# A three-mixer block on one core: the q, k projection with its two token parts side by side, and VectorE gating retention's outputs

## The chip, the cores and the metric

The kernel runs on one core of one Trainium2 chip. The time is device microseconds (us) of that core for one execution. The engines are TensorE (PE, with PEld for its weight loads), VectorE (DVE), ScalarE (ACT), GpSimd (POOL) and SyncE (SP), which here only issues DMAs.

## What is computed

256 tokens of width 1024 pass through a gated delta-net layer, a short-convolution layer, and then the second block, in which the change lies. Cut to what matters:

```python
proj = h @ w_in[l]                       # h: 256 x 1024
q, k, v, z_ret, u_val, u_gate, z_conv, g_a, g_b = jnp.split(proj, split_at, axis=-1)
qh = rotary(q.reshape(B, S, RET_HEADS, RET_HEAD_QK).astype(jnp.float32), positions)
kh = rotary(k.reshape(B, S, RET_HEADS, RET_HEAD_QK).astype(jnp.float32), positions) * RET_HEAD_QK ** -0.5
vh = v.reshape(B, S, RET_HEADS, RET_HEAD_V).astype(jnp.float32)
ret = head_groupnorm(retention_chunkwise(qh, kh, vh)).reshape(B, S, RET_V_DIM).astype(x.dtype)
y_a = (ret * jax.nn.silu(z_ret)) @ w_ret_out[l]
a = u_val * jax.nn.sigmoid(u_gate)
a = causal_depthwise_conv_2(a, conv_w[l], conv_b[l])     # 31 taps, 1024 channels
a = jax.nn.silu(layernorm(a, conv_ln_g[l], conv_ln_b[l]))
y_b = (a * jax.nn.silu(z_conv)) @ w_conv_out[l]
merged = jax.nn.sigmoid(g_a) * y_a + jax.nn.sigmoid(g_b) * y_b
```

## The kernel before

The weights stream in as chunks of 1 MB (`w_raw`), and every projection is a phase of such chunks, in the order of `PHASES`: ..., glu (8 chunks), qk (8), v (8), zret (8), zconv (4), gates (8), ret_out (8), conv_out (4), w_out (4). Products are made in float32 accuracy from three passes of float32r: each weight w and each activation h is kept as a high part and the rest (`w_hi`, `w_lo`, `hT_hi`, `hT_lo`), and PE adds w_hi·h_hi + w_hi·h_lo + w_lo·h_hi.

For each chunk, in two halves, ACT copies `w_raw` into `w_hi` (`split_hi`, line 1220), DVE subtracts to get `w_lo` (`split_lo`, line 1786), and PE multiplies. There are four half slots of each, so ACT's split of a half waits until PE is done with the same half two chunks earlier (`half_done`); DVE's split waits for ACT's (`hi_ready`), and PE's pass with `w_lo` waits for DVE's (`lo_ready`). In its program, each engine's step for chunk c first splits the second half of chunk c+1 and the first half of chunk c+2, and then does what the phase wants of chunk c (`each`).

PE has three ways to do a chunk. `chunk` (lines 677, 678, 686; phases qkv, qk, zconv) gives 16 + 16 + 16 matmuls of 256 columns, all into one PSUM bank `bank(j)`. `chunk_apart` (lines 695, 704; sc_in, glu) lets one matmul of 512 columns take `hT` high and low side by side, so that the halves land apart in two banks: 16 matmuls of 512 and 16 of 256; ACT then copies the low half out (`glu_part`) and DVE adds it. `wide_phase` and `wide_deep` (lines 727, 728, 734; v, zret, gates, ret_out ...) stream 512 weight columns, 24 matmuls of 512 for a chunk.

Between its splits DVE also does the 31-tap convolution, which is cut into 248 single operations (`conv_op`: lines 2396 and 2399, output `cv`, 128x256 each) and handed out by `conv_share(n)`: n of them in a step, until none is left. The shares by phase are written by hand: glu 22 in all, qk 3 a chunk, v 9 or 8, zret 7, zconv 8 and 5, gates 4 and then 10. After the last one DVE adds the channels up (`pair_sum`, `halves_sum`, output `ln_sum`, in the last step of gates), and PE takes the mean over them with a matmul (`layer_norm(0)`, line 1169) right behind the first chunk of ret_out; in PE's queue everything later stands behind it. POOL adds the first three channel pairs into `ln_sum` as they become ready (lines 1777, 1780).

In qk, DVE turns each chunk by the rotary angles straight out of PSUM (`rotate`: two multiplications into `rp`, one subtraction, one addition into `qkT`). PE's first matmuls on `qkT` (`scores`, line 1134) come behind the first chunk of v and wait for all eight. In zret, PE makes each head's retention outputs, DVE and ACT normalize them into `og`, and POOL multiplies `og` with the gates `zr` into `vt` (line 1773, two of 128x512 a head); in zconv PE transposes `vt` for ret_out.

Of the kernel before, what the change touches and what calls it, by code (L numbers as in the profile page):

```python
# [98 lines left out]
def build(nc, x_in, pre_norm_w, post_norm_w, gdn_w_in, gdn_conv_w, gdn_A_log, gdn_dt_bias, gdn_norm_w, gdn_w_out,  # L99
# [3 lines left out]
    with ctx:  # L103
# [146 lines left out]
        def bank(b, inner=SEQ):  # L250
            return psum[:, b, :].rearrange("p (a n) -> p a n", n=inner)
# [327 lines left out]
        def _(pe):  # L579
# [255 lines left out]
            def phase(name, a_hi, a_lo, beside=None, first=None, midway=None):  # L835

                g0 = FIRST[name]
                if name in ("sc_in", "glu"):
                    pe.wait_ge(bank_free, 4 + g0)

                def step(i):
                    for j in range(4):
                        ahead = isinstance(i, int) and i == 0
                        if ahead and j == 0 and first is not None:
                            first_chunk(g0, first)
                        elif ahead and j < 2 and midway is not None:
                            continue
                        elif name in ("sc_in", "glu"):
                            chunk_apart(i, g0, j, midway if ahead and j == 2 else None)
                        else:  # L850
                            chunk(i, g0, j, a_hi, a_lo, midway if ahead and j == 2 else None)
                        if beside is not None:
                            beside(4 * i + j)
                if beside is not None:
                    for i in range(COUNT[name] // 4):
                        step(i)
                elif midway is not None:
                    step(0)
                    with pe.Fori(1, COUNT[name] // 4) as i:
                        step(i)  # L860
                else:
                    loop(pe, COUNT[name] // 4, step)
# [263 lines left out]
            def scores(c):  # L1126

                if c == 0:
                    pe.wait_ge(rp_step, 2 * RH)
                if c < RH:  # L1130
                    b = psum[:, 4 + c, :]
                    for o, keys, queries in ((b[:, 0:SEQ], slice(0, P), slice(0, SEQ)), (b[:, SEQ:SEQ + P], slice(P, SEQ), slice(P, SEQ))):
                        for d in range(2):
                            mm = pe.matmul(o, qkT[:, KT + 2 * c + d, keys], qkT[:, 2 * c + d, queries], start=(d == 0), stop=(d == 1))  # L1134
                    mm.then_inc(sco_done, 1)
# [73 lines left out]
        def _(act):  # L1209
# [422 lines left out]
                act.wait_ge(bank_free, i * 4 + (4 + g + j - 1))  # L1632
                act.activation(glu_part[j % 2][:, :, :], psum[:, 2 * j:2 * j + 2, SEQ:2 * SEQ], ACT.Copy).then_inc(sc_act, 1)
            chunks("glu", glu_each, apart=True)
            chunks("qk")

            def tokens_out(dst, func):
                def each(i, j, done):
# [90 lines left out]
        def _(pool):  # L1729
# [36 lines left out]
            pool.wait_ge(yT_turned, KT)  # L1766
            pool.memset(ada_sum[:, :, :], 0.0).then_inc(ada_used, ADA)

            for n in range(NT * RH):
                h, t = n // NT, n % NT  # L1770
                pool.wait_ge(gn_ready, n + 1)
                vh = slice(h * RDV, (h + 1) * RDV)
                pool.tensor_tensor(vt[:, t, vh], og[t][:, :], zr[:, t, vh], ALU.mult).then_inc(rg_ready, 1)

            pool.wait_ge(rg_ready, NT * RH)
            pool.wait_ge(cv_step, CW * 4)
# [7 lines left out]
        def _(dve):  # L1784
# [655 lines left out]

            def rotate(i, j, done):
                c = 4 * i + j
                conv_share(3)
                dve.wait_ge(half_done, done)
                dve.tensor_tensor(rp1[:, :, :], bank(j), cos2, ALU.mult)
                dve.tensor_tensor(rp2[:, :, :], bank(j), sin2, ALU.mult).then_inc(bank_free, 1)
                dve.wait_ge(bank_free, 4 + FIRST["qk"] + c + 1)
                dve.tensor_tensor(qkT[:, 2 * c:2 * c + 1, :], rp1[:, 0:1, :], rp2[:, 1:2, :], ALU.subtract)
                dve.tensor_tensor(qkT[:, 2 * c + 1:2 * c + 2, :], rp2[:, 0:1, :], rp1[:, 1:2, :], ALU.add).then_inc(rp_step, 1)
                dve.wait_ge(rp_step, c + 1)  # L2450
            dve.wait_ge(bank_free, 4 + FIRST["qk"])
            chunks("qk", rotate, unroll=True)

            def decayed(i, j, done):
                c = 4 * i + j
                conv_share(9 if c < RH else 8)
                if c < RH:
                    dve.wait_ge(sco_done, c + 1)
                    dve.tensor_tensor(st[:, c, :], psum[:, 4 + c, 0:3 * P], decay[:, c, :], ALU.mult).then_inc(st_ready, 1)
# [4 lines left out]
            def group_scale(h):  # L2464
# [2 lines left out]
                dve.wait_ge(gn_rec, 2 * h + 1)  # L2467
                dve.scalar_tensor_tensor(out=gnm[:, :], in0=gmv[:, :, 0], scalar=-1.0, in1=grs[:, :], op0=ALU.mult, op1=ALU.mult).then_inc(gn_rec, 1)

            def group_norm(i, j, done):  # L2470
                n = 4 * i + j
                h, t = n // NT, n % NT
# [6 lines left out]
                if h:  # L2479
                    dve.wait_ge(gn_rec, 2 * h)  # L2480
                dve.bn_aggr(gmv[:, t, :], gst[:, t, :]).then_inc(gn_step, 1)
            chunks("zret", group_norm, unroll=True)

            def turned_pairs(i, j, done):
                if j == 0:
                    group_scale(RH - 1)
                conv_share(5 if j else 8)
                split_two(j)

            def split_two(q):  # L2490
# [16 lines left out]

            def last_pairs(i, j, done):
                c = 4 * i + j
                conv_share(10 if c else 4)  # L2510
                if c == COUNT["gates"] - 1:
                    dve.wait_ge(cv_step, CW * KT)
                    pair_sum(0, cv[:, KT - 2:KT, :], 2)
# [123 lines left out]
```

## Time and profile before

| | before |
|---|---|
| time, median of 3 runs (lowest to highest) | 838.21 us (837.5 to 838.33) |
| the profiled execution: its time / its span | 837.87 us / 836.1 us |
| PE busy | 827.8 us (99%) |
| DVE busy | 731.1 us (87%) |
| ACT busy | 500.2 us (60%) |
| POOL busy | 45.4 us (5%) |

The span runs from the first to the last instruction; 1.77 us of the execution's time lie around it. Busy time is the union of an engine's instructions. A matmul's duration contains its drain, so neighbours overlap: what a row of matmuls costs is read from the start of the first to the start of what follows. The same holds for DVE, by less than 0.1 us.

### The profile page before, as it was taken

What the parts mean: (1) busy time and instruction counts of PE and PEld (TensorE: products, weight loads), DVE (VectorE), ACT (ScalarE), POOL (GpSimd) and SP (SyncE); (2) the same over time, 40 slices, a digit from 0 to 9 for tenths busy, and PEclk for the clock granted to TensorE, in tenths of its full rate; (3) what the DMA queues carried; (4) which work ended last, traced back from release to release, by engine and by line L of the source; (5) the groups of instructions that cost most, each with busy time, mean ns of one, the idle gap of its engine ahead of it and who ended that gap; (6) DMA issues with size and microseconds to landing.
All of it is one profiled execution on the core that took longest, in us unless ns stands there. A gap on an engine that the chain in (4) does not pass through costs nothing.

```text
span 836.1 us, 13942 instructions
## 1 busy us (share of the span) xinstructions
PE 827.8 (99%) x5146; PEld 725.1 (87%) x5146; DVE 731.1 (87%) x1179; ACT 500.2 (60%) x804; POOL 45.4 (5%) x46
## 2 busy tenths in 40 slices
PE   8999999999999999999999999999999999999997
PEld 8999998789888888888888788998887798888886
DVE  7799899868877898888989979999999999988774
ACT  6899858576566555555565775333346675546743
POOL 0001101341100000000000000000001220000000
PEclk9999999999999999999999999999999999999999
DMA  9875675511875877777776656655454435564531
GB/s 277 256 253 169 211 245 174 146 38 45 278 232 179 261 262 263 257 256 252 238 257 218 221 185 213 202 184 169 155 198 151 152 118 200 186 231 171 188 115 50
DMA packets 129882, 164.13 MB, mean 196 GB/s; under 512 B 17407, under 2 KB 92199, under 8 KB 129703
## 3 DMA queue, kind: packets, MB, share of 16 engines
q1 hardware_dynamic: 129831, 163.45, 59.9%
q8 instruction: 33, 0.54, 0.3%
q14 instruction: 18, 0.15, 0.1%
HBM read 159.20 MB, written 4.23 MB: 195 GB/s over the span
## 4 chain that ended last, share of the span: by engine, by line
PE 98%; DVE 1%; DMA 1%; issue 0%; ACT 0%; DVEq 0%; SPq 0%; ACTq 0%
PE psum L695 16%; PE psum L727 14%; PE psum L728 14%; PE psum L734 14%; PE psum L704 8%; PE psum L677 6%; PE psum L686 6%; PE psum L678 6%; PE psum L1028 2%; PE psum L631 1%; PE psum L641 1%; PE psum L635 1%; PE psum L1033 1%; PE psum L915 1%; PE psum L1146 1%; PE psum L1134 1%
## 5 line engine op out<-in xcount | busy, mean ns | idle before, releaser
L1220 ACT ACTIVATE w_hi<-w_raw 128x1024 fp32r<-128x1024 f32 x255 | 266.6, 1061 | 188.2 <-PE psum L734 87.1
L1786 DVE TENSOR_TENSOR w_lo<-w_raw,w_hi 128x1024 fp32r<-128x1024 f32 x256 | 305.2, 1221 | 44.3 <-ACT w_hi L1220 42.2
L695 PE MATMUL psum<-hT,w_hi 128*128 128x512 f32 x576 | 138.9, 391 | 0.0
L695 PEld LDWEIGHTS psum<-hT,w_hi 128*128 128x128 f32 x576 | 105.4, 188 | 20.2
L727 PE MATMUL psum<-w_hi,hT 128*128 128x512 f32 x280 | 113.3, 405 | 0.0
L728 PE MATMUL psum<-w_hi,hT 128*128 128x512 f32 x280 | 109.3, 390 | 0.0
L2399 DVE SCALAR_TENSOR_TENSOR cv<-aP,par,cv 128x256 f32<-128x256 f32 x240 | 107.9, 519 | 0.0
L677 PE MATMUL psum<-hT,w_hi 128*128 128x256 f32 x432 | 107.4, 286 | 0.0
L678 PE MATMUL psum<-hT,w_hi 128*128 128x256 f32 x432 | 105.9, 283 | 0.0
L677 PEld LDWEIGHTS psum<-hT,w_hi 128*128 128x128 f32 x432 | 82.8, 192 | 0.4 <-issue 0.2
L678 PEld LDWEIGHTS psum<-hT,w_hi 128*128 128x128 f32 x432 | 82.9, 192 | 0.3 <-issue 0.2
L704 PEld LDWEIGHTS psum<-hT,w_lo 128*128 128x128 f32 x576 | 74.8, 191 | 3.3
L704 PE MATMUL psum<-hT,w_lo 128*128 128x256 f32 x576 | 76.1, 283 | 0.0
L727 PE MATMUL psum<-w_hi,yT_hi 128*128 128x512 f32 x192 | 75.8, 395 | 0.0
L734 PE MATMUL psum<-w_lo,hT 128*128 128x512 f32 x280 | 75.6, 390 | 0.0
L728 PE MATMUL psum<-w_hi,yT_lo 128*128 128x512 f32 x192 | 74.8, 390 | 0.0
L727 PEld LDWEIGHTS psum<-w_hi,hT 128*128 128x128 f32 x280 | 52.6, 188 | 12.0 <-issue 1.7
L728 PEld LDWEIGHTS psum<-w_hi,hT 128*128 128x128 f32 x280 | 52.6, 188 | 12.0 <-issue 1.7
L734 PEld LDWEIGHTS psum<-w_lo,hT 128*128 128x128 f32 x280 | 52.6, 188 | 11.2
L686 PE MATMUL psum<-hT,w_lo 128*128 128x256 f32 x432 | 60.6, 283 | 0.0
L686 PEld LDWEIGHTS psum<-hT,w_lo 128*128 128x128 f32 x432 | 55.7, 192 | 0.0
L734 PE MATMUL psum<-w_lo,yT_hi 128*128 128x512 f32 x192 | 52.7, 389 | 0.0
(341 smaller groups left out, 1108.6 us busy)
## 6 DMA issues: line engine op xcount, KB each, us to landing
w_raw<-in_w_in_dram SPq DMA_DIRECT2D x44, 1024.0 KB, 5.1
w_raw<-in_sc_w_in_dram SPq DMA_DIRECT2D x32, 1024.0 KB, 7.9
w_raw<-in_gdn_w_in_dram SPq DMA_DIRECT2D x23, 1024.0 KB, 7.1
ada<-in_w_ada_dram SPq DMA_DIRECT2D x24, 512.0 KB, 4.8
w_raw<-in_gdn_w_out_dram SPq DMA_DIRECT2D x8, 1024.0 KB, 5.5
w_raw<-in_sc_w_out_dram SPq DMA_DIRECT2D x8, 1024.0 KB, 6.4
w_raw<-in_w_ret_out_dram SPq DMA_DIRECT2D x8, 1024.0 KB, 5.1
w_raw<-in_w_conv_out_dram SPq DMA_DIRECT2D x4, 1024.0 KB, 5.1
```

Of the source, the lines that this page charges most:

```text
L677: pe.matmul(o[:, m, :], w_hi[s][:, k, mine], a_hi[:, ka, :], start=m == 0 and ka == 0, stop=False, skip_group_check=True)
L678: pe.matmul(o[:, m, :], w_hi[s][:, k, mine], a_lo[:, ka, :], start=False, stop=False, skip_group_check=True)
L686: mm = pe.matmul(o[:, m, :], w_lo[s][:, k, mine], a_hi[:, ka, :], start=False, stop=ka == KT - 1, skip_group_check=True)
L695: pe.matmul(o, w_hi[s][:, k, mine], hT[:, h * KH2 + k, :, :], start=h == 0 and k == 0, stop=False, skip_group_check=True)
L704: mm = pe.matmul(o, w_lo[s][:, k, mine], hT_hi[:, ka, :], start=False, stop=ka == KT - 1, skip_group_check=True)
L727: pe.matmul(psum[:, b + m, :], a_hi[:, ka, mine], wide(w_hi[s])[:, e, :], start=start and h == 0 and e == 0, stop=False, skip_group_check= ...
L728: pe.matmul(psum[:, b + m, :], a_lo[:, ka, mine], wide(w_hi[s])[:, e, :], start=False, stop=False, skip_group_check=True)
L734: mm = pe.matmul(psum[:, b + m, :], a_hi[:, k + 2 * h + e, mine], wide(w_lo[s])[:, e, :], start=False, stop=stop and h == 1 and e == 1, sk ...
L1028: mm = pe.matmul(b[:, a, :], left(a), right(a), start=True, stop=True)
L1220: act.activation((w_hi[half_slot(g, h)] if home is None else third_hi[half_slot(g, home)])[:, :, :], raw[slot][:, h * KH2:(h + 1) * KH2, : ...
L1786: return dve.tensor_tensor(o, whole, hi.bitcast(F32), ALU.subtract)
L2399: dve.scalar_tensor_tensor(out=cv[:, n, :], in0=src, scalar=w, in1=cv[:, n, :], op0=ALU.mult, op1=ALU.add).then_inc(cv_step, 1)
```

## The change

The qk phase goes from `chunk` to `chunk_apart`: per chunk 16 matmuls of 512 columns and 16 of 256 in place of 48 of 256, in two banks. ACT copies the low half of each chunk into `glu_part` (8 copies of 128x512), DVE adds it to the high half into `ug_sum`, and the rotary multiplications read that. The three `conv_op`s a chunk in qk are gone; the phases v and gates take them: v 8 and then 9 in place of 9 and then 8, gates 9 and then 10 to the end. The eight multiplications of `og` with `zr` go from POOL to DVE (`gated(h)`).

```diff
-                        elif name in ("sc_in", "glu"):
+                        elif name in ("sc_in", "glu", "qk"):
                             chunk_apart(i, g0, j, midway if ahead and j == 2 else None)
...
-                    pe.wait_ge(rp_step, 2 * RH)
+                    pe.wait_ge(rp_step, 4 * RH)
...
-            chunks("qk")
+            def beside_qk_2(i, j, done):
+                c, g = 4 * i + j, FIRST["qk"]
+                act.wait_ge(half_done, done)
+                act.wait_ge(bank_free, 4 + g + c - 1)
+                act.activation(glu_part[j % 2][:, :, :], psum[:, 2 * j:2 * j + 2, SEQ:2 * SEQ], ACT.Copy).then_inc(sc_act, 1)
+            chunks("qk", beside_qk_2, unroll=True)
...
-            for n in range(NT * RH):
-                h, t = n // NT, n % NT
-                pool.wait_ge(gn_ready, n + 1)
-                vh = slice(h * RDV, (h + 1) * RDV)
-                pool.tensor_tensor(vt[:, t, vh], og[t][:, :], zr[:, t, vh], ALU.mult).then_inc(rg_ready, 1)
...
             def rotate(i, j, done):
                 c = 4 * i + j
-                conv_share(3)
                 dve.wait_ge(half_done, done)
-                dve.tensor_tensor(rp1[:, :, :], bank(j), cos2, ALU.mult)
-                dve.tensor_tensor(rp2[:, :, :], bank(j), sin2, ALU.mult).then_inc(bank_free, 1)
+                dve.wait_ge(sc_act, 6 * KT - 2 + COUNT["glu"] - 2 + c + 1)
+                dve.tensor_tensor(ug_sum[:, :, :], psum[:, 2 * j:2 * j + 2, 0:SEQ], glu_part[j % 2][:, :, :], ALU.add).then_inc(bank_free, 1)
                 dve.wait_ge(bank_free, 4 + FIRST["qk"] + c + 1)
+                dve.tensor_tensor(rp1[:, :, :], ug_sum[:, :, :], cos2, ALU.mult)
+                dve.tensor_tensor(rp2[:, :, :], ug_sum[:, :, :], sin2, ALU.mult).then_inc(rp_step, 1)
+                dve.wait_ge(rp_step, 2 * c + 1)
...
-                conv_share(9 if c < RH else 8)
+                conv_share(8 if c < RH else 9)
...
+            def gated(h):
+                vh = slice(h * RDV, (h + 1) * RDV)
+                for t in range(NT):
+                    dve.wait_ge(gn_ready, NT * h + t + 1)
+                    dve.tensor_tensor(vt[:, t, vh], og[t][:, :], zr[:, t, vh], ALU.mult).then_inc(rg_ready, 1)
...
+                if n and t == 0:
+                    gated(h - 1)
...
+                if j == 0:
+                    gated(RH - 1)
...
-                conv_share(10 if c else 4)
+                conv_share(10 if c else 9)
```

DVE in the second chunk of qk, before (`cv` is a convolution operation, `w_lo` a split, the other four the rotation):

```order
L1786 TENSOR_TENSOR w_lo_59<-w_raw_52,w_hi_55 128x1024
L2399 SCALAR_TENSOR_TENSOR cv<-aP,par,cv 128x256 x3
L2445 TENSOR_TENSOR rp_168<-psum,trig 128x512
L2446 TENSOR_TENSOR rp_169<-psum,trig 128x512
L2448 TENSOR_TENSOR qkT<-rp_168,rp_169 128x256
L2449 TENSOR_TENSOR qkT<-rp_169,rp_168 128x256
```

The same place after:

```order
L1787 TENSOR_TENSOR w_lo_59<-w_raw_52,w_hi_55 128x1024
L2446 TENSOR_TENSOR ug_sum<-psum,glu_part_186 128x512
L2448 TENSOR_TENSOR rp_168<-ug_sum,trig 128x512
L2449 TENSOR_TENSOR rp_169<-ug_sum,trig 128x512
L2451 TENSOR_TENSOR qkT<-rp_168,rp_169 128x256
L2452 TENSOR_TENSOR qkT<-rp_169,rp_168 128x256
```

The three convolution operations are gone from here, and one addition has come in front of the rotation.

DVE in the fifth step of zret, before (`gst`, `gmv` are the statistics of the group norm):

```order
L2399 SCALAR_TENSOR_TENSOR cv<-aP,par,cv 128x256 x7
L2477 BN_STATS gst<-psum 128x6
L2481 BN_AGGR gmv<-gst 128x2
L1786 TENSOR_TENSOR w_lo_58<-w_raw_51,w_hi_54 128x1024
L1786 TENSOR_TENSOR w_lo_59<-w_raw_52,w_hi_55 128x1024
```

After, with a head's two multiplications ahead of the splits:

```order
L2400 SCALAR_TENSOR_TENSOR cv<-aP,par,cv 128x256 x6
L2397 TENSOR_SCALAR cv<-aP,par 128x256
L2486 BN_STATS gst<-psum 128x6
L2490 BN_AGGR gmv<-gst 128x2
L2477 TENSOR_TENSOR vt<-og_173,zr 128x512
L2477 TENSOR_TENSOR vt<-og_174,zr 128x512
L1787 TENSOR_TENSOR w_lo_58<-w_raw_51,w_hi_54 128x1024
L1787 TENSOR_TENSOR w_lo_59<-w_raw_52,w_hi_55 128x1024
```

The pair of `vt` has come from POOL's queue, once for each of the four heads.

DVE in the last two steps of gates, before (the rows of `ln_sum` are the sums that PE's mean waits for):

```order
L1786 TENSOR_TENSOR w_lo_60<-w_raw_52,w_hi_56 128x1024
L1786 TENSOR_TENSOR w_lo_57<-w_raw_49,w_hi_53 128x1024
L2399 SCALAR_TENSOR_TENSOR cv<-aP,par,cv 128x256
L1786 TENSOR_TENSOR w_lo_58<-w_raw_49,w_hi_54 128x1024
L1786 TENSOR_TENSOR w_lo_59<-w_raw_50,w_hi_55 128x1024
L2502 TENSOR_TENSOR ln_sum_189<-ln_sum_189,cv 128x512
L2506 TENSOR_TENSOR ln_sum_189<-ln_sum_189 128x256
```

After:

```order
L1787 TENSOR_TENSOR w_lo_60<-w_raw_52,w_hi_56 128x1024
L1787 TENSOR_TENSOR w_lo_57<-w_raw_49,w_hi_53 128x1024
L2400 SCALAR_TENSOR_TENSOR cv<-aP,par,cv 128x256 x10
L1787 TENSOR_TENSOR w_lo_58<-w_raw_49,w_hi_54 128x1024
L1787 TENSOR_TENSOR w_lo_59<-w_raw_50,w_hi_55 128x1024
L2400 SCALAR_TENSOR_TENSOR cv<-aP,par,cv 128x256 x10
L2515 TENSOR_TENSOR ln_sum_189<-ln_sum_189,cv 128x512
L2519 TENSOR_TENSOR ln_sum_189<-ln_sum_189 128x256
```

Ahead of the sums there stand 20 convolution operations in these two steps where there was one; over the whole gates phase it is 79 in place of 55.

## Rows read from the trace of the kernel before

**Rows 1.** The page's chain that ended last, shares by engine.

```profile
PE 98%; DVE 1%; DMA 1%; issue 0%; ACT 0%; DVEq 0%; SPq 0%; ACTq 0%
```

**Rows 2.** All of PE's waits: us in total, times, longest.

```profile
PE psum L879 <- DVE bg L2021: 1.3, 1, 1.3
...
PE psum L631 <- DVE hT L1976: 0.3, 1, 0.3
```

**Rows 3.** Timeline of PE, sc_in and qk: start, us, instructions.

```profile
329.19 3.82 PE L695 MATMUL psum<-hT,w_hi 128*128 128x512 f32 x16
...
334.75 3.82 PE L695 MATMUL psum<-hT,w_hi 128*128 128x512 f32 x16
...
521.54 0.28 PE L677 MATMUL psum<-hT,w_hi 128*128 128x256 f32 x1
...
567.62 0.40 PE L727 MATMUL psum<-w_hi,hT 128*128 128x512 f32 x1
```

**Rows 4.** Timeline of DVE, the first chunk of qk and its last end.

```profile
525.64 2.35 DVE L1786 TENSOR_TENSOR w_lo<-w_raw,w_hi 128x1024 fp32r<-128x1024 f32 x2
527.91 1.27 DVE L2399 SCALAR_TENSOR_TENSOR cv<-aP,par,cv 128x256 f32<-128x256 f32 x3
529.10 0.68 DVE L2445 TENSOR_TENSOR rp<-psum,trig 128x512 f32<-128x512 f32 x1
...
531.21 2.36 DVE L1786 TENSOR_TENSOR w_lo<-w_raw,w_hi 128x1024 fp32r<-128x1024 f32 x2
...
570.48 2.41 DVE L1786 TENSOR_TENSOR w_lo<-w_raw,w_hi 128x1024 fp32r<-128x1024 f32 x2
```

**Rows 5.** Timeline of PE: the first scores.

```profile
573.09 1.47 PE L1134 MATMUL psum<-qkT 128*128 128x256 f32 x8
```

**Rows 6.** Timelines of DVE and of POOL in zret and zconv.

```profile
634.23 1.23 DVE L1786 TENSOR_TENSOR w_lo<-w_raw,w_hi 128x1024 fp32r<-128x1024 f32 x1 [1.07 <-ACT w_hi L1220]
...
636.12 4.94 DVE L2399 SCALAR_TENSOR_TENSOR cv<-aP,par,cv 128x256 f32<-128x256 f32 x7
...
644.04 2.85 DVE L2399 SCALAR_TENSOR_TENSOR cv<-aP,par,cv 128x256 f32<-128x256 f32 x7
...
637.10 2.88 POOL L1773 TENSOR_TENSOR vt<-og,zr 128x512 f32<-128x512 f32 x2 [415.67 <-ACT og L1662]
...
694.84 1.33 POOL L1780 TENSOR_TENSOR ln_sum<-ln_sum,cv 128x512 f32<-128x512 f32 x1 [11.33 <-DVE cv L2399]
```

**Rows 7.** Timeline of DVE in gates, to its end.

```profile
702.89 2.35 DVE L1786 TENSOR_TENSOR w_lo<-w_raw,w_hi 128x1024 fp32r<-128x1024 f32 x2
...
709.01 4.04 DVE L2399 SCALAR_TENSOR_TENSOR cv<-aP,par,cv 128x256 f32<-128x256 f32 x10
712.96 2.35 DVE L1786 TENSOR_TENSOR w_lo<-w_raw,w_hi 128x1024 fp32r<-128x1024 f32 x2
...
742.81 0.70 DVE L2502 TENSOR_TENSOR ln_sum<-ln_sum,cv 128x512 f32<-128x512 f32 x1
...
743.88 2.35 DVE L1786 TENSOR_TENSOR w_lo<-w_raw,w_hi 128x1024 fp32r<-128x1024 f32 x2
```

**Rows 8.** Timeline of ACT: the split of gates' third chunk, first half.

```profile
700.28 1.06 ACT L1220 ACTIVATE w_hi<-w_raw 128x1024 fp32r<-128x1024 f32 x1 [1.16 <-PE psum L734]
```

**Rows 9.** Timeline of PE: the mean's matmul.

```profile
746.26 0.59 PE L1169 MATMUL psum<-ln_sum,const 128*128 128x256 f32 x2
```

**Rows 10.** Windows at the end: length, each engine's busy time, PE's granted clock.

```profile
831.00:832.00 1.00, 0.14 (x2) 0.00 (x0) 1.00 (x4) 0.77 (x3) 0.00 (x0) 1.00 0.46 174
...
833.00:834.00 1.00, 0.00 (x0) 0.00 (x0) 0.63 (x1) 0.00 (x0) 0.00 (x0) 1.00 0.18 68
834.00:835.00 1.00, 0.00 (x0) 0.00 (x0) 0.00 (x0) 0.00 (x0) 0.00 (x0) 0.51 1.01 377
```

**Rows 11.** PE's groups by form, of one form: count, busy us, mean ns.

```profile
L879 PE MATMUL psum<-bg 128*128 128x256 f32 x12 | 4.5, 549 | 1.3 <-DVE bg L2021 1.3
...
L1169 PE MATMUL psum<-ln_sum,const 128*128 128x256 f32 x2 | 0.6, 378 | 0.0
```

More of the change, by code:

```diff
@@ L2442, in rotate @@
                 c = 4 * i + j
-                conv_share(3)
                 dve.wait_ge(half_done, done)
-                dve.tensor_tensor(rp1[:, :, :], bank(j), cos2, ALU.mult)
-                dve.tensor_tensor(rp2[:, :, :], bank(j), sin2, ALU.mult).then_inc(bank_free, 1)
+                dve.wait_ge(sc_act, 6 * KT - 2 + COUNT["glu"] - 2 + c + 1)
+                dve.tensor_tensor(ug_sum[:, :, :], psum[:, 2 * j:2 * j + 2, 0:SEQ], glu_part[j % 2][:, :, :], ALU.add).then_inc(bank_free, 1)
                 dve.wait_ge(bank_free, 4 + FIRST["qk"] + c + 1)
+                dve.tensor_tensor(rp1[:, :, :], ug_sum[:, :, :], cos2, ALU.mult)
+                dve.tensor_tensor(rp2[:, :, :], ug_sum[:, :, :], sin2, ALU.mult).then_inc(rp_step, 1)
+                dve.wait_ge(rp_step, 2 * c + 1)
                 dve.tensor_tensor(qkT[:, 2 * c:2 * c + 1, :], rp1[:, 0:1, :], rp2[:, 1:2, :], ALU.subtract)
                 dve.tensor_tensor(qkT[:, 2 * c + 1:2 * c + 2, :], rp2[:, 0:1, :], rp1[:, 1:2, :], ALU.add).then_inc(rp_step, 1)
-                dve.wait_ge(rp_step, c + 1)
+                dve.wait_ge(rp_step, 2 * c + 2)
             dve.wait_ge(bank_free, 4 + FIRST["qk"])
```

## The prediction

> **What bounds the kernel now.** I read the chain of work that ended last first: 98% of the span is PE [rows 1]. Then PE's waits, which are the whole question here: 1.3 us at the very start, a few tenths later, and after the start of glu none [rows 2]. So from glu on PE runs its program without a gap. A change can win only by making that program shorter, and loses exactly what it makes PE wait. The next question is how late DVE comes, since every split with `w_lo` and the sums for the layer norm's mean are its work; for that I went down DVE's timeline beside PE's, phase by phase.
>
> In qk a chunk takes PE (567.62 - 521.54) / 8 = 5.76 us [rows 3], and DVE 531.21 - 525.64 = 5.57 us without a pause: two splits 2.27, three convolution operations 1.19, the rotation the rest [rows 4]. In gates DVE needs two splits and ten operations of 0.395 us (709.01 to 712.96 [rows 7]), 6.2 us for a chunk that PE does in about 5.4, and lives on the lead it came with. That lead ends at the mean: DVE's sums end at 743.88 [rows 7], PE reaches the mean's matmul at 746.26 [rows 9]. **The margin is 2.4 us.**
>
> **The change, part by part.**
>
> PE in qk. The form that the chunks take now stands in sc_in: 334.75 - 329.19 = 5.56 us a chunk [rows 3]. Eight chunks save 8 x (5.76 - 5.56) = 1.6 us; PE waits for nothing in either stretch, so this comes straight off the end. The bounds are 0.3 and 1.6 us. The saving is 12 ns for each of the 16 matmuls a chunk that fall away. The Trainium skill, "TensorE: Matmul & The Clock Gate", section "Wait — 56ns, not 53.3ns?", has a fixed cost of some 2.5 ns a matmul beyond its columns; by that alone 128 fewer would give 0.3 us, and the measured periods decide against it.
>
> ACT in qk gets eight copies of 128x512; it waits for PE there between its splits, so they cost nothing. The rotation of the last chunk now has a copy and an addition ahead of it, and no convolutions. Before, it ended at 570.48 [rows 4], 2.86 us behind PE's last product (567.62). After, behind that product come the copy (ACT, about 0.65, priced as DVE's 128x512 of 0.68), an addition and two multiplications of 0.6 each, and the two halves, 0.7 together: some 3.5 us, with a split that may lie in front 4. The scores begin 5.47 us behind the product [rows 5]. So the new wait of the scores costs nothing, by 1.5 us.
>
> DVE in qk: 5.57 - 1.19 + 0.6 = 5.0 us a chunk, under PE's 5.56. Here DVE now idles about half a microsecond a chunk. That idle time can't be carried on: its splits wait for ACT's, and ACT's for PE's slots, so DVE enters the v phase no further ahead than before. The 24 operations that stood in qk (9.5 us) don't vanish. With shorter and longer shares in v they net to nothing there, and all 24 land in gates: 79 in place of 55.
>
> The gates' product on DVE. Eight of 128x512, 0.62 us each (as the 128x512 addition of 0.70 less its overlap [rows 7]): 5.0 us more. But POOL's pairs were not free for DVE. Seven operations take 2.85 us with POOL quiet and 4.94 us beside a pair that takes POOL 2.88 us [rows 6]: 2.1 us lost a head, 8.4 in all. So this part gives DVE 3.4 us back by the end of zconv. The Trainium skill, "SBUF — State Buffer", section "Who interferes with whom", names the pair of ports that DVE and GpSimd share, an exclusive lock, as the only such conflict; the trace agrees, with the 4.94 us.
>
> The arrival in gates. Against before DVE has 3.4 us less to do since mid-v, and 4 operations (1.6 us) more: 1.8 us earlier. Its first pair of splits in gates, at 702.89 [rows 7], would start at 701.1, its second split at 702.2. It can't run before ACT's split of the same half, 700.28 + 1.06 = 701.34, which waits for PE [rows 8]. DVE had waits of up to 1.07 us in zret [rows 6] that a later DVE doesn't have, so it will be nearer to the floor: I take 701.4, bounds 701.3 and 702.2. (All places here are on the clock of before; PE's 1.6 us shift everything alike.)
>
> From there to the sums DVE has 15 splits of 1.14 (17.1), 79 operations of 0.395 (31.2), the sums 743.88 - 742.81 = 1.1, and, since POOL's second addition of 1.33 us now falls here too, 2.1 x 1.33 / 2.88 = 1.0: 50.4 us without a pause, to 751.8. As a check, the same prices for before, from 702.89: 16 splits, 55 operations and the sums give 18.2 + 21.7 + 1.1 = 41.0, and the trace has 743.88 - 702.89 = 41.0. **PE wants the sums at 746.26 and gets them at 751.8: it stands still for 5.5 us**, and all that follows in its queue with it. The bounds: 4.4, if POOL's addition costs DVE nothing, and 6.3 with the late arrival. On the way the last splits come close: that of ret_out's first chunk, second half, ends at about 745.5, some tenths late, within the same wait.
>
> Behind the mean. ACT's and DVE's further work on the layer norm hangs on the mean and on PE's halves, so it moves along with PE; nothing is paid twice.
>
> The clock. Such a pause is new. At the end of before PE's last product ends at 831.14; the granted clock is still 1.00 in 833 to 834, and 0.51 in 834 to 835 [rows 10], so an idle PE fell from 2.4 to 1.2 GHz after some 2.9 us. A pause of 5.5 us is longer. What it costs after: at the start of the kernel, with PE idle before, one form took 549 ns against 378 ns in the middle, for twelve matmuls [rows 11]; 12 x 0.17 = 2.1 us. I take 2.0, bounds 0 and, for a slow stretch half as long again, 3. The skill's same TensorE page, section "HAM oscillation — how this bites in real kernels", has the rule that a gap in PE's work brings the slow clock back; the rows of the end agree.
>
> **The sum**, against the profiled execution's own 837.87 us (836.1 of span and 1.77 around it): 837.87 - 1.6 + 5.5 + 2.0 = **843.8 us**. This execution lay 0.3 us under the median of 838.21, which I leave within the rounding.
>
> **The rivals.**
>
> *The pause, without the clock.* The fall of the clock depends on more than the length of one gap, and only the end of the kernel shows one. Without it 837.87 - 1.6 + 5.5 = 841.8 us. Chance 0.27; the forecast with the slow clock 0.58.
>
> *DVE is quicker than its shares say, and PE never waits.* This is the other side: 837.87 - 1.6 = 836.3, or 836.6 from the median. It decides at 5.5 us in gates: an operation would have to take 0.33 us in place of 0.395. With POOL's pairs gone DVE is the freer, and that speaks for it; but the 0.395 is from stretches in which POOL did nothing, and 15 splits of 1.14 with 79 operations are 48 us by themselves, more than the 44.9 from 701.4 to the mean. Chance 0.06, half of it for a wait small enough that the time comes out within 0.2% of before.
>
> *qk becomes the bound.* The new chain PE, ACT, DVE, PE through the copies might make PE wait in qk, or at the scores, if the last rotation comes more than 5.5 us behind PE. Glu has this chain in the same two buffers and no wait of PE. If it fell short by 1 us a chunk from the fifth on, that is 4 us on top, 847.8, though then DVE would also idle less in gates' lead. Chance 0.04.
>
> *The change doesn't shorten qk.* If the pairs of 256 columns and the 512 cost alike in this phase, the 1.6 us are missing and the pause stays: 845.4. The periods speak against it, chance 0.05.
>
> **How the numbers follow.** Two results differ measurably here when they are more than 0.2% (1.7 us) apart. The likeliest case has 843.8. Its own range is 837.87 - 1.6 + 4.4 + 0 = 840.7 to 837.87 - 0.3 + 6.3 + 2 = 845.9. That takes in the case without the clock, and leaves out the quick DVE, the bound in qk and the outer corners: 840.8 to 845.8. Faster by over 0.2% (under 836.5) needs the quick DVE and the whole saving: 0.03. Within 0.2% (836.5 to 839.9): 0.06, a pause of under 3.5 us with a clock that holds. Slower: 0.91.
>
> **What the changed kernel's profile would show.** In qk 5.56 us a chunk on PE and pauses of DVE waiting for ACT's copies. In zret seven operations in 2.85 us beside every head. In gates DVE without a pause from the second split on, and 79 operations. At the mean's matmul one wait of PE on DVE's `ln_sum`, about 5.5 us, the only long one; behind it a stretch of ret_out at a granted clock of 0.5, or not. If that wait is absent, the forecast is wrong; if it is there and the time isn't, the saving in qk or the clock is what I have mis-sized.

## The result, and the profile after

The changed kernel takes 844.53 us, the median of six executions between 843.5 and 845.46. The kernel before, beside it on the same chip, takes 838.17 us (six, 837.5 to 838.56). The ratio is 1.0077, with a 95% interval of 1.0064 to 1.009: slower by 6.4 us. The forecast was 843.8 us, within a range of 840.8 to 845.8 that holds the time.

The profiled execution of the changed kernel took 844.91 us, with 842.8 us of span. I read it as I read the one before. First PE's waits (the engine and the line that waited, what it waited for, us in total, times, longest):

```profile
PE psum L1169 <- DVE ln_sum L2519: 5.1, 1, 5.1
PE psum L879 <- DVE bg L2022: 1.3, 1, 1.3
PE psum L884 <- DMA vecs<-in_pre_norm_w_dram: 0.5, 1, 0.5
PE psum L873 <- DVE xn L1870: 0.4, 1, 0.4
```

Against [rows 2] there is one new row, and it is the first: the mean's matmul waits 5.1 us for DVE's sums. No other wait behind the start of glu is as long as half a microsecond. The page's chain of work that ended last says the same in another way; in [rows 1] DVE had 1%:

```profile
PE 92%; DVE 7%; DMA 1%; ACT 0%; issue 0%; DVEq 0%; SPq 0%; ACTq 0%
```

DVE's 7% are some 59 us, and 50 of them are its run through gates: it works there without a pause up to the sums (750.18 - 699.82, below), so the chain follows it back to where it last waited. PE lost only 5.6 us of that. A share of the chain isn't the loss.

PE's timeline in the stretches of [rows 3] and [rows 9] (start, us, engine, line, operation, output and inputs, shape, count, and in brackets the idle time before it):

```profile
521.54 3.82 PE L695 MATMUL psum<-hT,w_hi 128*128 128x512 f32 x16
...
527.10 3.82 PE L695 MATMUL psum<-hT,w_hi 128*128 128x512 f32 x16
...
566.07 0.40 PE L727 MATMUL psum<-w_hi,hT 128*128 128x512 f32 x1
...
571.54 1.47 PE L1134 MATMUL psum<-qkT 128*128 128x256 f32 x8
...
744.03 1.20 PE L734 MATMUL psum<-w_lo,yT_hi 128*128 128x512 f32 x4
...
750.31 1.22 PE L1169 MATMUL psum<-ln_sum,const 128*128 128x256 f32 x2 [5.08 <-DVE ln_sum L2519]
...
756.15 0.39 PE L727 MATMUL psum<-w_hi,yT_hi 128*128 128x512 f32 x1
```

Both kernels begin qk at 521.54. The changed one begins v at 566.07 in place of 567.62: 1.55 us saved, (566.07 - 521.54) / 8 = 5.57 us a chunk. From there to the mean PE needs 750.31 - 566.07 = 184.24 us, where it needed 746.26 - 567.62 = 178.64: 5.60 us lost, 5.08 of them in the one wait. The mean's two matmuls themselves take 1.22 us there, twice what they take in a kernel without the pause (0.59 in the experiments below).

DVE's timeline at the places that the prediction named:

```profile
564.88 1.23 DVE L1787 TENSOR_TENSOR w_lo<-w_raw,w_hi 128x1024 fp32r<-128x1024 f32 x1
566.47 1.23 DVE L1787 TENSOR_TENSOR w_lo<-w_raw,w_hi 128x1024 fp32r<-128x1024 f32 x1 [0.36 <-ACT w_hi L1220]
567.61 0.68 DVE L2446 TENSOR_TENSOR ug_sum<-psum,glu_part 128x512 f32<-128x512 f32 x1
...
570.45 2.36 DVE L1787 TENSOR_TENSOR w_lo<-w_raw,w_hi 128x1024 fp32r<-128x1024 f32 x2
...
634.57 2.85 DVE L2400 SCALAR_TENSOR_TENSOR cv<-aP,par,cv 128x256 f32<-128x256 f32 x7
...
699.82 1.23 DVE L1787 TENSOR_TENSOR w_lo<-w_raw,w_hi 128x1024 fp32r<-128x1024 f32 x1 [0.96 <-ACT w_hi L1220]
700.97 3.65 DVE L2400 SCALAR_TENSOR_TENSOR cv<-aP,par,cv 128x256 f32<-128x256 f32 x9
...
745.04 4.04 DVE L2400 SCALAR_TENSOR_TENSOR cv<-aP,par,cv 128x256 f32<-128x256 f32 x10
749.11 0.69 DVE L2515 TENSOR_TENSOR ln_sum<-ln_sum,cv 128x512 f32<-128x512 f32 x1
749.84 0.42 DVE L2519 TENSOR_TENSOR ln_sum<-ln_sum 128x256 f32<-128x256 f32 x1
750.18 3.49 DVE L1787 TENSOR_TENSOR w_lo<-w_raw,w_hi 128x1024 fp32r<-128x1024 f32 x3
```

The last pause of DVE is in front of the second split of gates, at 699.82; from there it works through to the sums, which are done at 750.18. Seven convolution operations take 2.85 us beside every head, since POOL does nothing there any more; in [rows 6] the groups beside a pair took 4.94 us.

Last, the windows around the pause (stretch, length, busy us of PE, PEld, DVE, ACT and POOL, then the granted clock, the DMA share and GB/s):

```profile
748.00:749.00 1.00, 0.00 (x0) 0.00 (x0) 1.00 (x3) 0.00 (x0) 0.00 (x0) 0.99 0.54 209
749.00:750.00 1.00, 0.00 (x0) 0.00 (x0) 0.93 (x3) 0.00 (x0) 0.00 (x0) 0.50 0.00 0
...
754.00:755.00 1.00, 1.00 (x4) 0.81 (x3) 0.00 (x0) 0.00 (x0) 0.00 (x0) 0.50 1.07 418
755.00:756.00 1.00, 1.00 (x4) 0.77 (x4) 0.00 (x0) 0.00 (x0) 0.00 (x0) 0.60 1.03 401
756.00:757.00 1.00, 1.00 (x6) 0.84 (x5) 0.00 (x0) 0.59 (x1) 0.00 (x0) 1.00 1.09 393
```

PE's last product before the pause ended at about 745.2. At 749 the granted clock fell to 0.50 (1.2 GHz) and came back to 2.4 GHz between 755 and 756, so PE worked from 750.3 to about 755.8 at half its speed. From the mean to the next half's first matmul it took 756.15 - 750.31 = 5.84 us. Before, the same stretch went from the mean at 746.26 [rows 9] to this row:

```profile
749.46 0.39 PE L727 MATMUL psum<-w_hi,yT_hi 128*128 128x512 f32 x1
```

That is 3.20 us, so the clock cost 2.64 us.

The parts meet: 837.87 - 1.55 + 5.60 + 2.64 + 0.34 (what lies around the span, 2.11 us now and 1.77 then) = 844.90 us.

### The profile page after: what moved, and what is told of

Read it like the earlier page. It is cut to its first block, busy times and chain, and to the rows that moved or that the text cites. A ratio compares the mean times of both kernels' runs of the same rounds, so it can differ in the third digit from the quotient of the medians.

```text
span 842.8 us, 13701 instructions
## 1 busy us (share of the span) xinstructions
PE 829.5 (98%) x5018; PEld 720.2 (85%) x5018; DVE 732.5 (87%) x1195; ACT 503.3 (60%) x812; POOL 33.8 (4%) x38
## 4 chain that ended last, share of the span: by engine, by line
PE 92%; DVE 7%; DMA 1%; ACT 0%; issue 0%; DVEq 0%; SPq 0%; ACTq 0%
PE psum L695 19%; PE psum L727 12%; PE psum L728 12%; PE psum L734 12%; PE psum L704 10%; PE psum L677 4%; PE psum L686 4%; PE psum L678 4%; DVE cv L2400 4%; PE psum L1028 2%; DVE w_lo L1787 2%; PE psum L631 1%; PE psum L641 1%; PE psum L635 1%; PE psum L1033 1%; PE psum L915 1%
## 5 line engine op out<-in xcount | busy, mean ns | idle before, releaser
L695 PE MATMUL psum<-hT,w_hi 128*128 128x512 f32 x704 | 169.4, 391 | 0.0
L695 PEld LDWEIGHTS psum<-hT,w_hi 128*128 128x128 f32 x704 | 129.0, 188 | 24.8
L2400 DVE SCALAR_TENSOR_TENSOR cv<-aP,par,cv 128x256 f32<-128x256 f32 x240 | 97.8, 476 | 0.0
L704 PEld LDWEIGHTS psum<-hT,w_lo 128*128 128x128 f32 x704 | 91.2, 191 | 3.9
L704 PE MATMUL psum<-hT,w_lo 128*128 128x256 f32 x704 | 92.7, 283 | 0.0
L677 PE MATMUL psum<-hT,w_hi 128*128 128x256 f32 x304 | 76.0, 288 | 0.0
L678 PE MATMUL psum<-hT,w_hi 128*128 128x256 f32 x304 | 74.5, 283 | 0.0
L677 PEld LDWEIGHTS psum<-hT,w_hi 128*128 128x128 f32 x304 | 58.2, 192 | 0.4 <-issue 0.2
L678 PEld LDWEIGHTS psum<-hT,w_hi 128*128 128x128 f32 x304 | 58.3, 192 | 0.3 <-issue 0.2
L734 PEld LDWEIGHTS psum<-w_lo,yT_hi 128*128 128x128 f32 x192 | 36.5, 190 | 8.2 <-DVE w_lo L1787 0.5
L727 PEld LDWEIGHTS psum<-w_hi,yT_hi 128*128 128x128 f32 x192 | 36.6, 191 | 7.6
```

The lines of the kernel that those rows point to most:

```text
L677: pe.matmul(o[:, m, :], w_hi[s][:, k, mine], a_hi[:, ka, :], start=m == 0 and ka == 0, stop=False, skip_group_check=True)
L678: pe.matmul(o[:, m, :], w_hi[s][:, k, mine], a_lo[:, ka, :], start=False, stop=False, skip_group_check=True)
L695: pe.matmul(o, w_hi[s][:, k, mine], hT[:, h * KH2 + k, :, :], start=h == 0 and k == 0, stop=False, skip_group_check=True)
L704: mm = pe.matmul(o, w_lo[s][:, k, mine], hT_hi[:, ka, :], start=False, stop=ka == KT - 1, skip_group_check=True)
L727: pe.matmul(psum[:, b + m, :], a_hi[:, ka, mine], wide(w_hi[s])[:, e, :], start=start and h == 0 and e == 0, stop=False, skip_group_check= ...
L734: mm = pe.matmul(psum[:, b + m, :], a_hi[:, k + 2 * h + e, mine], wide(w_lo[s])[:, e, :], start=False, stop=stop and h == 1 and e == 1, sk ...
```

## The experiments

Theory A, the prediction's: 24 operations moved from qk into gates make DVE's sums late, PE stands at the mean, and the clock falls. Theory B: the loss comes from the new form itself or from the products on VectorE, and the wait at the mean is only where it shows. Theory C: the wait alone counts, the clock costs nothing. Ten kernels tell them apart. The kernel before ran beside them in three sets, with medians of 838.0 us (17 executions; the first three experiments and the one with the products back on GpSimd), 837.95 us (15; the ones with two and with three operations a chunk) and 837.76 us (27; the last four).

### The mean's matmul one chunk later

```diff
-                if c == 0:
+                if c == 1:
                     pe.wait_ge(ln_sum_step, 4)
```

> The changed kernel, with PE taking the layer norm's mean one chunk of ret_out later (behind its second chunk in place of its first). Nothing else moves: DVE still has 79 operations in gates. If the loss is PE's wait for DVE's sums: in the changed kernel they end at 750.18, and PE now reaches the mean at 744.7 + 5.4 = 750.1, so the wait of 5.1 us shrinks to under 0.5, the clock does not fall, and of the change only its saving in qk is left: 837.87 - 1.55 + 0.3 = 836.6 us, 0.1 to 0.2% under before. If DVE's splits are what comes late (a rival: DVE is simply overloaded in gates), PE waits for lo parts instead and the time stays above 840. The variance's matmul follows two chunks later and has some 4 us of margin, so no new wait there.

It took 838.93 us (11 executions, 838.23 to 840.24), ratio 1.0011 (1.0002 to 1.002). So moving the one wait by one chunk takes back 5.6 of the 6.4 us. By A the wait and the clock are 5.60 + 2.64 = 8.2 us, and 836.6 was expected: some 2.3 us are left. Most of that is a wait of PE that the profiled execution (838.42 us) shows in a new place:

```profile
750.87 1.20 PE L734 MATMUL psum<-w_lo,yT_hi 128*128 128x512 f32 x4 [1.64 <-DVE w_lo L1787]
```

DVE's timeline says why:

```profile
749.25 0.42 DVE L2519 TENSOR_TENSOR ln_sum<-ln_sum 128x256 f32<-128x256 f32 x1
749.60 3.49 DVE L1787 TENSOR_TENSOR w_lo<-w_raw,w_hi 128x1024 fp32r<-128x1024 f32 x3
```

The split of ret_out's second chunk stands in DVE's queue behind the sums. A late DVE is late for the splits too: PE's pause is 3.5 us shorter than at the mean, but it isn't gone, and my expectation had overlooked it. During these 1.64 us the clock stayed at 1.00.

### PE kept busy during the wait

```diff
                 if c == 0:
+                    for _ in range(22):
+                        pe.matmul(psum[:, 5, :], yT_hi[:, 0, 0:P], yT_hi[:, 0:2, :], start=True, stop=True)
                     pe.wait_ge(ln_sum_step, 4)
```

The 22 matmuls go to a bank of PSUM from which nothing reads them. PE then gets to the mean just as late, but not from standing still: the time without the clock's part.

> The changed kernel, with 22 matmuls of 512 columns into an unused PSUM bank in front of PE's wait for the sums; they add work that nothing reads, about 22 x 0.228 = 5.0 us, just what PE stands still. The sums come as late as before. If the fall of the clock is a cost of its own, on top of the pause (5.6 us of pause, 2.6 us of slow stretch in the changed kernel's trace), the clock now stays at 1.00 and the first chunk half behind the mean takes 3.2 us, not 5.8: 844.5 - 2.6 = 841.9 us. If the slow half chunk has another cause (late weights, DVE), the time stays at 844.5. If the fillers last longer than the pause, up to 0.5 us more.

It took 842.44 us (5 executions, 842.05 to 843.72), ratio 1.0052 (1.0039 to 1.0066). Windows of its profiled execution, the fill and what follows it:

```profile
746.00:751.00 5.00, 5.00 (x24) 4.12 (x23) 4.97 (x12) 1.06 (x1) 0.00 (x0) 1.00 0.69 210
...
752.00:754.00 2.00, 2.00 (x10) 1.65 (x9) 2.00 (x3) 0.00 (x0) 0.00 (x0) 1.00 0.03 8
```

The clock stays at 1.00, and the kernel is 844.53 - 842.44 = 2.1 us faster for doing more. The stretch behind the mean is in PE's timeline (the mean's matmuls now stand on line 1171):

```profile
751.63 0.70 PE L1171 MATMUL psum<-ln_sum,const 128*128 128x256 f32 x2
...
754.93 0.39 PE L727 MATMUL psum<-w_hi,yT_hi 128*128 128x512 f32 x1
```

It takes 3.30 us in place of 5.84. Theory C falls: the idle time and the clock are two separate costs. By the medians the clock is 2.1 us, by the traces 2.5 to 2.6.

### One operation a chunk stays in qk

`conv_share` does a given number of convolution operations; those not done earlier remain for gates. Eight stay in qk, 71 are left for gates.

```diff
                 c = 4 * i + j
+                conv_share(1)
                 dve.wait_ge(half_done, done)
                 dve.wait_ge(sc_act, 6 * KT - 2 + COUNT["glu"] - 2 + c + 1)
```

> The changed kernel, with one convolution operation in each step of qk, so 8 fewer at the end of gates (71, the last step has 2). By the count of operations: the sums come 8 x 0.395 = 3.2 us sooner, the pause falls from 5.6 to 2.4 us, and DVE in qk takes 5.0 + 0.4 = 5.4 us a chunk, still under PE's 5.57. If the clock holds over a pause of 2.4 us: 837.87 - 1.55 + 2.4 = 838.7 us; if it falls as well, about 841. If instead the gates' product on DVE is what costs, the time stays near 844.5; if DVE in qk is already the bound there, PE waits in qk and the time rises again.

It took 840.9 us (7 executions, 839.26 to 841.36), ratio 1.0029 (1.0018 to 1.004). PE's timeline, and its windows:

```profile
746.89 1.22 PE L1169 MATMUL psum<-ln_sum,const 128*128 128x256 f32 x2 [1.92 <-DVE ln_sum L2520]
```

```profile
745.00:746.00 1.00, 0.00 (x0) 0.00 (x0) 0.97 (x3) 0.99 (x1) 0.00 (x0) 1.00 0.79 123
746.00:747.00 1.00, 0.11 (x1) 0.11 (x1) 0.97 (x3) 0.07 (x1) 0.00 (x0) 0.96 1.03 393
747.00:748.00 1.00, 1.00 (x3) 0.82 (x4) 1.00 (x2) 0.00 (x0) 0.00 (x0) 0.50 1.06 412
...
750.00:751.00 1.00, 1.00 (x5) 0.82 (x4) 0.24 (x1) 0.00 (x0) 0.00 (x0) 0.84 0.88 338
```

Eight operations fewer in gates are 8 x 0.395 = 3.2 us, and the wait went from 5.08 to 1.92, by 3.16. Operation for operation, the wait is DVE's work in gates. The clock fell here too, just as PE came back to work, although it had stood for only 1.9 us; that was the upper of the two times expected, about 841. One of the seven executions took 839.26 us, near the lower one (838.7), with a mean granted clock of 0.999 over the whole execution; the six others took 840.27 to 841.36 us with 0.996 or 0.997. So in that one the clock may have held; it has no trace that could show it.

### Two operations a chunk stay in qk

The same line with `conv_share(2)`.

> The changed kernel with two convolution operations in each step of qk (16 in all, 63 left for gates). At the mean nothing is late any more (pause 5.6 - 16 x 0.395 < 0). In qk DVE now takes 5.05 + 0.8 = 5.85 us a chunk against PE's 5.57 and falls 2.3 us behind over the phase; the last rotation then ends about 5.5 us behind PE's last product, where the scores stand 5.47 behind it. So a wait of 0 to 0.7 us at the scores: 836.3 to 837.0 us. If the new form of qk has room for DVE's operations in any number, no wait.

It took 839.75 us (11 executions, 838.14 to 841.43), ratio 1.0015 (1.0005 to 1.0026). I expected 836.3 to 837.0. The wait at the mean is gone, but PE's timeline has another, at the scores:

```profile
573.75 1.57 PE L1134 MATMUL psum<-qkT 128*128 128x256 f32 x8 [1.97 <-DVE qkT L2453]
```

Two neighbouring chunks of qk on DVE show it:

```profile
564.99 0.68 DVE L2447 TENSOR_TENSOR ug_sum<-psum,glu_part 128x512 f32<-128x512 f32 x1
...
570.89 0.68 DVE L2447 TENSOR_TENSOR ug_sum<-psum,glu_part 128x512 f32<-128x512 f32 x1
```

A chunk takes DVE 5.90 us, more than PE's 5.57, so it falls behind through qk. The 0.90 us by which this passes the prediction's 5.0 are more than two operations (0.79): the work without any is 5.1 to 5.2. The eleven executions spread over 3.3 us, where all but one of the kernel before's in this set lie between 837.2 and 839.6. In the profiled one (838.96 us) the clock held. Three of the five executions over 839.9 us have a mean granted clock of 0.997, and none of the kernel before's in this set is under 0.998. That makes a fall of the clock in some of them likely; it isn't shown, since the slower ones have no trace.

### All of the shares as before

The changed kernel with before's numbers: three a chunk in qk, before's shares in v, four in the first chunk of gates.

```diff
+                conv_share(3)
                 dve.wait_ge(half_done, done)
...
-                conv_share(8 if c < RH else 9)
+                conv_share(9 if c < RH else 8)
...
-                conv_share(10 if c else 9)
+                conv_share(10 if c else 4)
```

> The changed kernel with the convolution's shares as before the change: 3 in each step of qk, 9 and 8 in v, 4 and 10 in gates. At the mean nothing is late. In qk DVE takes 5.05 + 1.2 = 6.25 us a chunk against 5.57 and falls 5.4 us behind: the last rotation ends some 8.7 us behind PE's last product, the scores want it at 5.47, so PE waits about 3.2 us there, and the clock may fall as it did over a pause of 1.9 us: 839.5 us, 841.5 with the slow clock. If DVE's lead holds (rival: no wait at the scores), moving the operations was needless and it gives the saving alone, 836.3.

It took 843.53 us (5 executions, 842.78 to 844.66), ratio 1.0064 (1.0049 to 1.0079). The mechanism was as expected, and the higher of the two times (841.5) was 2 us short. PE's timeline and its windows:

```profile
576.24 2.93 PE L1134 MATMUL psum<-qkT 128*128 128x256 f32 x8 [3.83 <-DVE qkT L2453]
```

```profile
575.00:576.00 1.00, 0.00 (x0) 0.00 (x0) 0.97 (x3) 0.23 (x1) 0.00 (x0) 0.83 0.68 262
576.00:577.00 1.00, 0.77 (x2) 0.68 (x3) 0.97 (x2) 0.00 (x0) 0.00 (x0) 0.50 0.00 0
```

The wait moved from the mean to the scores, and the eight matmuls of the first scores, at a halved clock, take 2.93 us in place of 1.47. PE waited 3.83 us there, and 0.7 us for two splits ahead of it, where 3.2 in all was expected. The new form of qk does need room on DVE: of the 24 operations only the eight of the experiment with one a chunk fit in without a wait there.

### The products back on GpSimd

The changed kernel with the loop over `n` (the gates' products) back in GpSimd's queue, as in before, and without the two calls of `gated`.

> The changed kernel, with the eight multiplications of og and zr back in POOL's queue. By my price of POOL beside DVE (2.1 us lost for a head's pair, 8.4 in all, against 5.0 us of own work) DVE comes 3.4 us later out of zconv, of which 1.0 us is taken up by its wait for ACT at the first splits of gates: sums 2.4 us later, pause 8.0 us, clock down as well: about 847 us. If the product on DVE is the cause of the loss (rival), it goes back to about 837. If POOL beside DVE costs nothing in the end, it stays at 844.5.

It took 847.04 us (4 executions, 845.92 to 848.34), ratio 1.0105 (1.009 to 1.0121): 2.5 us slower than the changed kernel. PE's waits at and before the mean in gates and ret_out:

```profile
PE psum L1169 <- DVE ln_sum L2520: 5.1, 1, 5.1
...
PE psum L734 <- DVE w_lo L1792: 1.2, 3, 0.5
```

And in zret, on DVE:

```profile
636.55 4.93 DVE L2405 SCALAR_TENSOR_TENSOR cv<-aP,par,cv 128x256 f32<-128x256 f32 x7
```

The seven operations take 4.93 us again. The pause at the mean was expected to be 8.0 us, and it is 5.1 as in the changed kernel. The sums do come 3.7 us later (753.85 against 750.18), but that shows in waits for splits ahead of the mean: between the last split that PE needs and the sums lies a fixed piece of DVE's work (5.14 us in both traces), so a DVE that is later still holds up PE at the split already. VectorE's products are thus a gain, the opposite of what theory B says of them.

### Two parts of the change, each alone on the kernel before

The products moved to VectorE in the kernel before, with its shares and its form of qk:

> The kernel before with one part of the change: the eight multiplications of og and zr on DVE. PE never waited in before and DVE gains 3.4 us net by zconv, so the sums come about 1.5 us sooner, ahead of PE by some 4 us; PE's program is the same: 838.0 us, no difference. If the product on DVE costs PE something (rival: the transposes of vt wait for it), it is slower by what PE waits.

It took 837.57 us (11 executions, 836.9 to 839.09), ratio 0.9998 (0.9989 to 1.0007): no difference. Its profile has no wait at the mean. The freed time of DVE is real: the sums end at 744.1 and the mean begins at 747.51, 3.4 us ahead where it was 2.4. But there is nobody on the path who wants it.

The shares of the changed kernel alone in the kernel before (no operation in qk, v and gates as changed), with the old form of qk and the products on GpSimd:

```diff
-                conv_share(3)
                 dve.wait_ge(half_done, done)
...
-                conv_share(9 if c < RH else 8)
+                conv_share(8 if c < RH else 9)
...
-                conv_share(10 if c else 4)
+                conv_share(10 if c else 9)
```

> The kernel before with another part alone: the convolution's shares as in the change (none in qk, 8 and 9 in v, 79 in gates), with PE's qk in 48 matmuls and the product on POOL. The sums then end as late as with the product on POOL in the changed kernel, and qk saves nothing: 847.0 + 1.6 = 848.6 us. If the pause needs the new form of qk (rival: the copies and additions are what delays DVE), it is near 838.

It took 847.82 us (4 executions, 845.84 to 849.83), ratio 1.0119 (1.0099 to 1.014). PE's waits have the mean's again:

```profile
PE psum L1169 <- DVE ln_sum L2505: 5.1, 1, 5.1
```

This is theory A alone: three numbers that say where the operations stand, and nothing else of the change, cost 847.82 - 837.76 = 10.1 us, more than the whole change. The other two parts together take 847.82 - 844.53 = 3.3 us of it back. Theory B falls for the loss of the changed kernel. The third part alone, the new form of qk with everything else as before, was not run; with the products on VectorE beside it, that is the kernel with all of the shares as before, where the new form's price shows at the scores and not at the mean.

### Two versions without a wait

One operation a chunk in qk, and the mean one chunk later (the first and the third experiment together):

> Both of the earlier half measures: one operation in each step of qk (71 in gates) and the mean taken one chunk later. With the mean later alone PE still waited 1.6 us, for the split of ret_out's second chunk, second half, which stands behind DVE's sums; 8 operations fewer bring that split 3.2 us sooner, so no wait is left and the clock holds: 836.3 us. If some 1.6 us of wait stay, the split is not held up by the operations, and the time is 838.

It took 836.96 us (11 executions, 836.15 to 838.24), ratio 0.999 (0.9981 to 0.9999). The sums on DVE, and PE at the mean, in its profiled execution (836.28 us):

```profile
745.91 0.42 DVE L2520 TENSOR_TENSOR ln_sum<-ln_sum 128x256 f32<-128x256 f32 x1
```

```profile
749.76 0.59 PE L1169 MATMUL psum<-ln_sum,const 128*128 128x256 f32 x2
```

The sums are ready 3.5 us before PE wants them, and the mean's matmuls take 0.59 us.

One operation a chunk in qk and more of them in v and zret, with the mean where it was:

```diff
+                conv_share(1)
                 dve.wait_ge(half_done, done)
...
-                conv_share(8 if c < RH else 9)
+                conv_share(9)
...
-                conv_share(7)
+                conv_share(8)
                 dve.wait_ge(ro_done, n + 1)
...
-                conv_share(10 if c else 9)
+                conv_share(8)
```

> The changed kernel with the convolution operations dealt out where DVE waits for ACT: 1 a chunk in qk, 9 a chunk in v, 8 in zret, zconv as it was, and the remaining 59 in gates (8 a chunk) in place of 79. DVE's waits in v and zret come to some 3 us in the changed kernel's trace and take up most of what is added there. From gates' second split at about 700: 15 splits 17.1, 59 operations 23.3, the sums 1.1 give 741.7, with POOL's addition or a later arrival up to 743.5; PE is there at 744.7. No pause, clock at 1.00, only the saving in qk left: 836.3 us, about 0.2% under before. If the saving in qk is not real (rival), 838; if DVE without a rest comes late elsewhere, PE waits for splits in zret or gates and the time is above 838.

It took 836.98 us (11 executions, 835.9 to 838.98), ratio 0.9992 (0.9983 to 1.0001). Here the sums lie 2.7 us ahead, DVE first and PE below:

```profile
741.95 0.43 DVE L2520 TENSOR_TENSOR ln_sum<-ln_sum 128x256 f32<-128x256 f32 x1
```

```profile
744.98 0.59 PE L1169 MATMUL psum<-ln_sum,const 128*128 128x256 f32 x2
```

Two ways of making room give the same time, 0.8 us under the kernel before, at the edge of what can be told apart. That is what the change is worth when nobody waits for its price. The saving in qk is whole in both traces: the phase takes 44.53 and 44.54 us where it took 567.62 - 521.54 = 46.08. Against it stands what lies around the span. In every execution of the kernels that have both the new form and the products on VectorE that is 2.1 to 2.2 us; in every one of the kernel before and of the kernels that have one of the two or neither, it is 1.7 to 1.9. What takes the 0.35 us isn't shown. So 1.55 - 0.35 = 1.2 us are left, which the intervals of both ratios hold (up to 1.6 and up to 1.4 us).

## Why the prediction was right, point by point

**The bound.** PE's program with the first wait at the mean was the right frame: of the 6.4 us all but a few tenths are the terms that were read from it. The profiled execution lies 1.1 us over the forecast: 0.64 is the clock, 0.34 what lies around the span, and the rest the wait and the saving.

**The saving in qk.** Forecast 1.6 us, 1.55 measured. Pairs of 256 columns merged into one matmul of 512 save 12 ns a matmul here as they do in [rows 3]. That the shortening reaches the end when PE waits for nothing is shown less sharply, by the two versions without a wait: 0.8 us in the medians. The 1.55 us lie at the upper end of the bounds of 0.3 and 1.6.

**The rotation.** Forecast that the last one ends 3.5 to 4 us behind PE's product; it was 570.45 - 566.07 = 4.4. The scores began at 571.54, so the slack was 1.1 us in place of 1.5. No wait, as forecast.

**DVE in qk.** Forecast 5.0 us of work a chunk, measured 5.57 - 0.36 = 5.2. The added addition takes 0.72 us to the start of what follows (567.61 to 568.33), where 0.6 was counted. And the pauses of DVE in qk are waits for ACT's `w_hi`, as the working had it, not for ACT's copies, as the list of what the profile would show had it. The longer work cost nothing here, but it is why two operations a chunk don't fit.

**The products.** The trade of 5.0 us of products for 8.4 us of lost time stands: 2.85 us beside every head, and 2.5 us slower with the products back on GpSimd. As forecast, the second addition on GpSimd now fell into DVE's work; two operations beside it took 1.63 us to the start of what follows (711.60), where 0.65 is their own without GpSimd (0.33 each at 604.21), so it cost the 1.0 us of the sum:

```profile
709.97 1.71 DVE L2397 TENSOR_SCALAR cv<-aP,par 128x256 f32<-128x256 f32 x2
```

**The arrival and the sums.** On the clock of before, the second split was forecast at 701.4 as the floor that ACT sets, and came at 699.82 + 1.55 = 701.37, waiting for ACT. The sums were forecast for 751.8 and came at 750.18 + 1.55 = 751.73. This step made the forecast: a count of operations from the last pause onward, tested on the kernel before.

**The wait.** Forecast 5.5 us, measured 5.60 with the tenths in front of it. The experiment with eight operations fewer (3.16 us for 3.2) and the one with the shares alone show the cause.

**The clock.** The term that was mis-sized: forecast 2.0 us, 2.64 in the trace. The forecast counted twelve matmuls that lose 0.17 us each. Twelve was the number at the start of the kernel, and nothing tied it to the slow stretch behind the mean; that the result came as near as 0.64 us was in part luck. The windows give a better price: PE began again at 750.3, the clock was back at about 755.8 (0.60 in the window from 755), and of 5.5 us at half the clock half is lost, some 2.7 us. The rival without the clock (841.8) was wrong for this kernel. The wait with a busy PE took 842.44 us, which is that rival's case made on purpose.

**The rest.** What lies around the span was taken over as 1.77 us and came out 0.34 us longer. The experiments show that this isn't noise of one execution but belongs to the changed kernel; the sum had it at nothing.

## What to carry to other kernels

When operations are moved out of a phase to make it fit, follow them to where they land: add up the engine's work from its last pause to the next thing that another engine waits for, and test the same sum on the kernel before, where the answer is known. The same 24 operations made the kernel 6 to 10 us slower where they all landed in front of the mean, and cost nothing when eight stayed and either the rest lay where DVE had slack or the wait stood one chunk later; with all 24 in gates and only the wait moved, 0.9 us were left. Leaving them all in qk was no way out either, since the new form needs the room there (5.6 us slower). A pause of the matmul engine can be charged twice, once for its length and once for the clock afterwards: behind a wait of 1.92 us that happened, behind one of 1.97 us in another kernel it didn't.

## What the runs showed of the hardware

A short pause can bring the slow clock, and doesn't always. With the wait of 1.92 us the granted clock fell to 0.50 at 747, when PE had just begun again, and PE worked at 1.2 GHz until between 750 and 751. In two other profiled executions pauses of 1.64 and 1.97 us left it at 1.00. With 3.83 us and 5.08 us it fell. The Trainium skill, "TensorE: Matmul & The Clock Gate", section "HAM oscillation — how this bites in real kernels", warns of pauses above a certain length, which is longer than 1.92 us; here the measured fall decides. What decides between the short cases stays open: each has one trace only. Matmuls whose product nobody read, put into the pause, kept the clock at 1.00.

GpSimd's work slows DVE's convolution operations beside it, but by less than the whole of GpSimd's time. A pair of 128x512 takes GpSimd 2.88 us and costs DVE 2.1, about 0.73 of it; the single addition of 1.33 us cost 1.0. In the set with the products on GpSimd again, that loss was 4.93 - 2.85 = 2.08 us a head.
